# Scores in three single-pass products of high and low parts, and one softmax scaling moved to ScalarE, in a four-layer transformer kernel

## The reference

```python
def diff_attend(q, k, v, lam):
    s = jnp.einsum('bqhmd,bkhmd->bhmqk', q, k).astype(jnp.float32) * (DIFF_QK ** -0.5)
    p = jax.nn.softmax(s, axis=-1)
    a = p[:, :, 0] - lam * p[:, :, 1]
    return jnp.einsum('bhqk,bkhd->bqhd', a.astype(v.dtype), v)
```

## Time and profile before

| | |
|---|---|
| median of 3 runs | 3357.74 us (3357.29 to 3358.83) |
| the profiled execution | 3358.63 us, its span 3357.3 us |
| busy | PE 97%, weight loads 82%, DVE 64%, ACT 41%, POOL 7% |
| mean granted clock of TensorE | 0.99 |
| head loop of layer 2 | 1968.4 to 2112.6 us |
| head loop of layer 3 | 2814.2 to 2925.8 us |
| DMA | 100 GB/s on average |

### The profile page before, as it was taken

One profiled execution on the slowest core, in us unless ns is written; L12 is line 12 of the kernel. 1 busy time (PEld: TensorE's weight loads), 2 busy tenths in 40 slices (PEclk: granted clock), 3 DMA queues, 4 the chain that ended last, 5 costly groups with the idle time before them and its releaser, 6 DMA issues. The chain is left out here.

```text
span 3357.3 us, 45065 instructions
## 1 busy us (share of the span) xinstructions
PE 3243.3 (97%) x17830; PEld 2767.6 (82%) x17830; DVE 2150.5 (64%) x3560; ACT 1389.9 (41%) x2242; POOL 221.0 (7%) x336
## 2 busy tenths in 40 slices
PE   7998999999999999999999999999999999999998
PEld 5787789999978888878878886889999987688887
DVE  5678477888665545558788466476777865654444
ACT  5478353333444324342223345353333444542332
POOL 0001100000000000003111000100000010010001
PEclk9999999999999999999999999999999999999999
DMA  6500124444221221226664211113333231122232
GB/s 242 201 23 1 38 74 128 144 132 140 91 93 46 101 78 47 88 76 200 204 200 167 85 45 51 38 67 116 113 104 110 83 103 57 44 88 94 94 101 76
DMA packets 98689, 334.39 MB, mean 100 GB/s; under 512 B 11872, under 2 KB 16768, under 8 KB 95024
## 3 DMA queue, kind: packets, MB, share of 16 engines
q1 hardware_dynamic: 77072, 252.63, 22.4%
q0 software_dynamic: 21408, 78.88, 7.4%
HBM read 329.37 MB, written 2.10 MB: 99 GB/s over the span
## 5 line engine op out<-in xcount | busy, mean ns | idle before, releaser
L1245 ACT ACTIVATE WH<-WR 128x1024 fp32r<-128x1024 f32 (+3 forms) x516 | 443.1, 863 | 916.0 <-PE PS L638 679.5
L1862 DVE TENSOR_TENSOR WL<-WR,WH 128x1024 fp32r<-128x1024 f32 (+3 forms) x516 | 507.9, 986 | 449.1 <-ACT WH L1245 447.9
L638 PE MATMUL PS<-HH,WH 128*128 128x512 f32 x1608 | 544.2, 373 | 8.7 <-DVE WK L2295 3.4
L638 PE MATMUL PS<-HH,WL 128*128 128x512 f32 x1608 | 539.7, 370 | 0.0
L638 PE MATMUL PS<-HL,WH 128*128 128x512 f32 x1608 | 539.2, 369 | 0.0
L638 PE MATMUL PS<-D,WH 128*128 128x512 f32 x1648 | 420.9, 361 | 1.5 <-DVE D L2319 1.4
L638 PEld LDWEIGHTS PS<-HH,WH 128*128 128x128 f32 x1608 | 280.6, 189 | 69.6 <-issue 9.9
L638 PEld LDWEIGHTS PS<-HL,WH 128*128 128x128 f32 x1608 | 279.4, 189 | 52.8 <-issue 1.0
L638 PEld LDWEIGHTS PS<-HH,WL 128*128 128x128 f32 x1608 | 279.7, 189 | 52.2
L638 PEld LDWEIGHTS PS<-D,WH 128*128 128x128 f32 x1648 | 275.7, 188 | 52.6 <-DVE D L2319 3.2
L638 PE MATMUL PS<-D,WL 128*128 128x512 f32 (+1 forms) x824 | 257.3, 360 | 0.0
(11 more groups left out here) (377 smaller groups left out, 6042.5 us busy)
## 6 DMA issues: line engine op xcount, KB each, us to landing
WR<-in_win SPq DMA_DIRECT2D x176, 512.0 KB, 3.5
AT<-in_adat POOLq DMA_DIRECT2D x144, 512.0 KB, 3.9
WR<-in_wret SPq DMA_DIRECT2D x64, 512.0 KB, 3.7
WR<-in_zin SPq DMA_DIRECT2D x36, 512.0 KB, 3.5
WR<-in_wdn SPq DMA_DIRECT2D x32, 448.0 KB, 3.4
WR<-in_wdn SPq DMA_DIRECT2D x48, 256.0 KB, 2.7
WR<-in_wdn SPq DMA_DIRECT2D x32, 320.0 KB, 3.0
AR<-in_ada SPq DMA_DIRECT2D x8, 1024.0 KB, 19.1
```

The source lines that it names most:

```text
L638: mm = PE.matmul(dst[:, a:b], w(u)[:, k * P:(k + 1) * P], h[:, k, a:b], start=(k == 0 and i == 0), stop=(k == nk - 1 and i == 2))
L1245: AC.activation(M.hi(u), M.raw(u), COPY).then_inc(*on.up("w_hi", u))
L1862: VE.tensor_tensor(M.lo(u), M.raw(u), M.hi(u).bitcast(F32), ALU.subtract).then_inc(*on.up("w_lo", u))
```

## The change

The scores are made of three fp32r products per map, over new tiles: `QH`, `KH` (high parts, copied by ACT in `score_high`) and `QL`, `KL` (low parts, subtracted by DVE, in the place of q and k themselves). The four copies stand among ACT's refills ahead of the head loop, the four subtractions on DVE behind its last refill, and PE's first scores wait for the last of these. `NIL` shrinks to one column that is read repeatedly. In the head loop the scaling of map 0 goes from DVE (L2702) to ACT as a copy with a scale, between the copy of the output and the exponentials of the next block; the reciprocal stands ahead of the next block's reads of the scores.

```diff
--- before.py
+++ after.py
@@ -389,6 +389,7 @@
         t = self.tile
         Z = self.top
         self.Z = t("Z", [P, 12, T])
+        at = Z + 10 * 4 * T
         self.DK = t("DK", [P, 2, T])
         self.OD = t("OD", [P, 2, T])
         self.top -= 8 * T
@@ -417,9 +418,13 @@
         self.top = top
         self.dP = [[t(f"dP{m}{i}", [P, T]) for i in range(3 - m)] for m in range(2)]
         self.dPT = [t(f"dPT{i}", [P, 6, P]) for i in range(3)]
-        self.NIL = t("NIL", [P, T])
-        self.top = Z + 96 * 1024
+        self.NIL = t("NIL", [P, 1])
+        self.QH = t("QH", [P, 2, T], F32R)
+        self.KH = t("KH", [P, 2, T], F32R)
         self.CN = [t("CN0", [P, 2, S])]
+        self.top = at
+        self.QL = t("QL", [P, 2, T], F32R)
+        self.KL = t("KL", [P, 2, T], F32R)
         for i, at in enumerate((Z + 8 * T, Z + 24 * T, self.HI6)):
             self.top = at
             self.CN.append(t(f"CN{i + 1}", [P, 2, S]))
@@ -1159,18 +1164,19 @@
             if j < len(heads):
                 q, h, nm, m0 = heads[j]
                 if j == 0:
-                    PE.wait_ge(*on("roped", (l, 3)))
+                    PE.wait_ge(*on("roped", (l, "low", 3)))
                 w, c0 = nm * P, m0 * P
                 rows = [slice(64 * (h % 2) + 32 * mp, 64 * (h % 2) + 32 * mp + 32) for mp in range(2)]
                 for a in range(0, w, 512):
                     e = min(w, a + 512)
-                    for mp, r in enumerate(rows):
-                        if j and a == 0:
-                            PE.wait_ge(*on("d_max", (l, j - 1, mp)))
-                        mm = PE.matmul(PS[mp][:, a:e], M.Z[r, 10 + h // 2, q * P:(q + 1) * P], M.DK[r, h // 2, c0 + a:c0 + e],
-                                       start=True, stop=True, tile_position=(r.start, 0))
-                        if e == w:
-                            mm.then_inc(*on.up("d_scores", (l, j, mp)))
+                    for i, (qs, ks) in enumerate(((M.QH, M.KH), (M.QL, M.KH), (M.QH, M.KL))):
+                        for mp, r in enumerate(rows):
+                            if j and a == 0 and i == 0:
+                                PE.wait_ge(*on("d_max", (l, j - 1, mp)))
+                            mm = PE.matmul(PS[mp][:, a:e], qs[r, h // 2, q * P:(q + 1) * P], ks[r, h // 2, c0 + a:c0 + e],
+                                           start=i == 0, stop=i == 2, tile_position=(r.start, 0))
+                            if e == w and i == 2:
+                                mm.then_inc(*on.up("d_scores", (l, j, mp)))
             j = step - 4
             if j >= 0 and j % 2 == 0:
                 q, h, nm, m0 = heads[j]
@@ -1732,8 +1738,18 @@
             if p == 5:
                 AC.wait_ge(*on("lambda_dots", l))
                 AC.activation(M.LAM[:, 0:2], M.LAM[:, 0:2], EXP).then_inc(*on.up("lambda_exp", l))
-        for v in range(2):
-            refill(u + 4 + ROWS_AT + v)
+
+        def score_high(t):
+            dst, src, w = (M.QH, Z[:, 10 + t, 0:n], n) if t < 2 else (M.KH, M.DK[:, t - 2, :], T)
+            AC.wait_ge(*on("roped", (l, t)))
+            AC.activation(dst[:, t % 2, 0:w], src, COPY).then_inc(*on.up("z_copied", (l, "high", t)))
+
+        score_high(0)
+        refill(u + 4 + ROWS_AT)
+        score_high(1)
+        score_high(2)
+        refill(u + 5 + ROWS_AT)
+        score_high(3)
         AC.wait_ge(*on("product", u + 3 + ROWS_AT))
         for i in range(3):
             AC.activation(flat(M.DV, 2 * i, 2 * i + 2), bank(PS, 4 + i), COPY).then_inc(*on.up("dv_copied", (l, i)))
@@ -1790,6 +1806,11 @@
                 AC.wait_ge(*on("d_values", (l, j // 2)))
                 AC.activation(M.OD[:, :, q * P:(q + 1) * P], PS[2][:, T:T + 2 * P].rearrange("p (t q) -> p t q", t=2),
                               COPY).then_inc(*on.up("d_out", (l, q)))
+            j = step - 1
+            if 0 <= j < len(heads):
+                p = M.dP[0][j % 3][:, 0:heads[j][2] * P]
+                AC.wait_ge(*on("step", ("d_sum", l, j)))
+                AC.activation(p, p, COPY, scale=M.dRL[:, j % 4, 0:1]).then_inc(*on.up("d_exp", (l, j, "first")))
             j = step
             if j < len(heads):
                 w = heads[j][2] * P
@@ -2659,6 +2680,10 @@
         refill(u + 4 + ROWS_AT)
         rope(3)
         refill(u + 5 + ROWS_AT)
+        for t in range(4):
+            dst, hi, src, w = (M.QL, M.QH, Z[:, 10 + t, 0:n], n) if t < 2 else (M.KL, M.KH, M.DK[:, t - 2, :], T)
+            VE.wait_ge(*on("z_copied", (l, "high", t)))
+            VE.tensor_tensor(dst[:, t % 2, 0:w], src, hi[:, t % 2, 0:w].bitcast(F32), ALU.subtract).then_inc(*on.up("roped", (l, "low", t)))
 
         def low(k, a, b, src, event):
             VE.wait_ge(*on("mix_hi", event))
@@ -2681,6 +2706,12 @@
         VE.wait_ge(*on("step", ("nil", l)))
         heads, pace = diff_heads(l), PACE[l]
         for at in range(6 * pace + 7):
+            j = at - 1
+            if 0 <= j < len(heads):
+                sums = M.dRL[:, j % 4, :]
+                VE.wait_ge(*on("d_exp", (l, j, 1)))
+                step(VE.reciprocal(sums, sums), ("d_sum", l, j))
+                VE.tensor_tensor(sums[:, 1:2], sums[:, 1:2], LAM[:, 2:3], ALU.mult).then_inc(*on.up("step", ("d_second", l, j)))
             j = at
             if j < len(heads):
                 w = heads[j][2] * P
@@ -2690,16 +2721,14 @@
                     VE.wait_ge(*on("d_prob", (l, j - 2)))
                 for mp in range(2):
                     VE.wait_ge(*on("d_scores", (l, j, mp)))
-                    VE.tensor_tensor_reduce(M.dP[mp][j % (3 - mp)][:, 0:w], PS[mp][:, 0:w], M.NIL[:, 0:w], -(32 ** -0.5), 3e38,
+                    VE.tensor_tensor_reduce(M.dP[mp][j % (3 - mp)][:, 0:w], PS[mp][:, 0:w], M.NIL[:, 0:1].to_broadcast([P, w]), -(32 ** -0.5), 3e38,
                                             ALU.add, ALU.min, M.dNM[:, j % 4, mp:mp + 1]).then_inc(*on.up("d_max", (l, j, mp)))
             j = at - 1
             if 0 <= j < len(heads):
                 w = heads[j][2] * P
                 p0, p1, sums = M.dP[0][j % 3], M.dP[1][j % 2], M.dRL[:, j % 4, :]
-                VE.wait_ge(*on("d_exp", (l, j, 1)))
-                step(VE.reciprocal(sums, sums), ("d_sum", l, j))
-                VE.tensor_tensor(sums[:, 1:2], sums[:, 1:2], LAM[:, 2:3], ALU.mult)
-                step(VE.tensor_scalar(p0[:, 0:w], p0[:, 0:w], sums[:, 0:1], None, ALU.mult), ("d_first", l, j))
+                VE.wait_ge(*on("d_exp", (l, j, "first")))
+                VE.wait_ge(*on("step", ("d_second", l, j)))
                 VE.scalar_tensor_tensor(p0[:, 0:w], p1[:, 0:w], sums[:, 1:2], p0[:, 0:w], ALU.mult,
                                         ALU.add).then_inc(*on.up("d_prob", (l, j)))
             if 0 < at <= 6 * pace and at % pace == 0:
```

## The result

| | before | after |
|---|---|---|
| median | 3357.29 us of 5 (3353.09 to 3358.83) | 3370.9 us of 5 (3369.95 to 3372.72) |
| profiled span | 3357.3 us | 3369.9 us |
| step loop of layer 2 | 144.2 us | 150.9 us |
| step loop of layer 3 | 111.6 us | 117.6 us |

The changed kernel takes 1.0041 times as long (95% interval 1.0029 to 1.0053), 13.6 us more. The two head loops are longer by 6.7 and 6.0 us, which is all of the difference between the two spans.

A forecast was written before the change was run, and what follows sets the result against it. PE, in certain steps ACT, was taken to set the pace. Shorter scores -5.6, low parts +4.5 and +4.0, clock +2.7 and scaling on ACT +1.7 made +7.3 us: 3365.0 us, range 3359.5 to 3371.

The forecast's parts named there:

- the first rival: Wide score blocks: weight loads for the same rows are not hidden, 1.76 us a block, 3376 us in all; chance 6%.

The follow-up runs named there:

- experiment 6: kernel 3 with all three passes of map 0 ahead of those of map 1, chunk by chunk: 3353.53 us, ratio 0.9987 to before.
- kernel 1: The changed kernel with k's last high part on ACT and the four low parts on DVE ahead of each engine's second refill: 3357.33 us, ratio 1.000 to before.
- kernel 3: The changed kernel with high and low parts ahead of the last refills, and map 0's scaling back on DVE: 3354.05 us, ratio 0.9983 to before.

## What to carry to other kernels

When an operand is split in two, the second half has a place in the order of its own: put it where the engines wait anyway (here one refill earlier), since the same four subtractions cost 13.6 us in the one place, clock and all, and nothing that can be measured in the other. Before work moves to an engine with idle time, read what its neighbours in the order wait for, and follow who is queued behind the one that now waits for it, over more than one engine. Shorter work on the busiest engine pays only in the steps where nobody else's copy is awaited; here an exchange of two copies on ACT raised what it paid from 1.1 to 2.4 us in eleven blocks of layer 3.

## What the runs showed of the hardware

- Products on different groups of 32 rows ran side by side although three products stood between the partners in the order (experiment 6): 12 products of 32 rows took 1.25 us in either order. So the sentence ahead of the prediction that each engine takes its instructions strictly in the written order does not hold for PE's starts in such a block. The Trainium skill, page "TensorE: Matmul & The Clock Gate", section "The mechanism", states that matmuls start in the order of the program; the records of kernel 6 and its 1.25 us speak against it for products of different row groups.
- A weight load for rows that the running product uses was hidden behind it: passes of 512 columns started 0.23 us apart and passes of 256 columns 0.12, each with new weights for the same 32 rows. The list in the same section of the Trainium skill has such loads overlap only when the row group differs; by that rule the block would have been the 1.76 us of the first rival, and it was 1.25. (The sentence above that list also lets a load go ahead when it is for the background weight buffer, which the measured block does not contradict.)
- A pair of plain fp32 products of 512 columns, one of each map, costs 0.86 us as two halves of 0.43; three pairs of fp32r passes over the same columns cost about 0.7 at 0.23 each. With the 256 columns behind them (0.43 against 0.36) that is the whole of what the three passes gain, 0.23 us per wide block.
- After idle times of 5.9 and 5.4 us on PE the granted clock stood at 0.50 for 10.2 and 6.8 us; 42 small products in the gap kept it at 1.00 and took 5.5 us off the time, without the first scores coming earlier. After 1.51 us it stood at 0.50 in kernel 1 and at 1.00 in kernel 3.
